# Expert weights in row chunks: up ahead of gate, accumulation over two chunks

## The reference, cut to what matters

```
def expert_block(args):
    ids, e = args
    xb = tokens_pad[ids]
    hgu = xb @ w_gu_l[e] + b_gu_l[e]
    gate = jnp.minimum(hgu[:, :D_EXPERT], SWIGLU_LIMIT)
    up = jnp.clip(hgu[:, D_EXPERT:], -SWIGLU_LIMIT, SWIGLU_LIMIT)
    act = gate * jax.nn.sigmoid(SWIGLU_ALPHA * gate) * (up + 1.0)
    return act @ w_dn_l[e] + b_dn_l[e]
```

## Time and profile before

| | us |
|---|---|
| median of 3 runs | 2111.39 (2110.61 to 2113.88) |
| the profiled execution | 2111.9 |
| its span | 2110.2 |
| first expert matmul | 780.1 |
| PE busy in the span | 1855.6 (88%) |
| DVE busy | 1531.5 (73%) |
| ACT busy | 1336.0 (63%) |

### The profile page before, as it was taken

How to read it: one execution, slowest core, us unless ns; L and a number is a source line. 1 busy time by engine, 2 the same in 40 slices (tenths; PEclk the granted TensorE clock), 3 DMA queues, 4 the chain that set the end, 5 groups by cost and what they waited for, 6 DMA issues and landing times.

```text
span 2110.2 us, 56858 instructions
## 1 busy us (share of the span) xinstructions
PE 1855.6 (88%) x23915; PEld 1646.0 (78%) x23915; DVE 1531.5 (73%) x1917; ACT 1336.0 (63%) x1751; POOL 309.8 (15%) x330
## 2 busy tenths in 40 slices
PE   5998898897779957899999999999999989899993
PEld 3585775575554547899999999999989989899893
DVE  5465566528862276788878887888888988989884
ACT  5354443227752244777777777778778787787883
POOL 2000000000000047311222122222221011111110
PEclk9999999999999959999999999999999999999996
DMA  6104111062124167899999999999999999999975
GB/s 187 39 25 128 31 31 35 26 174 67 61 99 163 60 251 276 272 305 327 316 337 328 336 315 336 343 340 350 349 344 349 365 363 358 367 354 366 362 236 180
DMA packets 246163, 503.91 MB, mean 239 GB/s; under 512 B 12967, under 2 KB 27603, under 8 KB 246017
## 3 DMA queue, kind: packets, MB, share of 16 engines
q1 hardware_dynamic: 228736, 459.91, 61.7%
q0 software_dynamic: 16192, 38.64, 7.5%
q10 hardware_dynamic: 1152, 4.19, 0.5%
HBM read 467.62 MB, written 37.38 MB: 239 GB/s over the span
## 4 chain that ended last, share of the span: by engine, by line
PE 61%; DVE 16%; issue 10%; ACT 8%; POOL 2%; DMA 2%; DVEq 0%; ACTq 0%; POOLq 0%; SPq 0%
PE PS L1577 34%; PE PS L1363 8%; PE PS L1369 6%; DVE RP L1192 5%; PE PS L1509 4%; PE PS L1415 4%; ACT RP L773 4%; DVE RW L1260 2%; ACT RT L809 2%; POOL table L555 2%; DVE RT L1274 1%; DVE RX L1070 1%; DVE RX L1105 1%; PE PS L1641 1%; DVE RW L1264 1%
## 5 line engine op out<-in xcount | busy, mean ns | idle before, releaser
L1577 PE MATMUL PS<-RT,RP 128*128 128x128 f16 (+3 forms) x18432 | 1130.2, 224 | 78.4 <-DVE RT L1274 59.3
L1577 PEld LDWEIGHTS PS<-RT,RP 128*128 128x128 f16 x18432 | 1120.5, 98 | 88.0 <-issue 67.0
L1192 DVE SCALAR_TENSOR_TENSOR RP<-RP 128x2048 f16<-128x2048 f32 x256 | 582.7, 2288 | 163.5 <-ACT RP L773 156.8
L773 ACT ACTIVATE RP<-RP 128x2048 f16<-128x2048 f32 x256 | 486.2, 1911 | 19.7 <-PE PS L1577 16.0
L1192 DVE SCALAR_TENSOR_TENSOR RP<-RX,RP 128x2048 f16<-128x2048 f32 x128 | 292.3, 2283 | 0.0
L773 ACT ACTIVATE RP<-RX 128x2048 f16<-128x2048 f32 x128 | 243.3, 1901 | 4.7 <-PE PS L1577 4.0
L1363 PE MATMUL PS<-RX,RW 128*128 128x512 f16 x768 | 172.7, 383 | 0.8 <-DVE RX L897 0.8
L663 ACT ACTIVATE RP<-PS 128x512 f32<-128x512 f32 (+1 forms) x56 | 33.3, 596 | 185.1 <-PE PS L1363 100.9
L1363 PEld LDWEIGHTS PS<-RX,RW 128*128 128x128 f16 x768 | 75.8, 99 | 87.3 <-issue 3.4
L804 ACT ACTIVATE RT<-RW 128x256 f16<-128x256 f32 (+3 forms) x128 | 55.3, 432 | 138.2 <-DVE RW L1268 134.1
L809 ACT ACTIVATE RT<-PS,bcur 128x128 f32<-128x128 f32 (+3 forms) x256 | 83.2, 384 | 84.5 <-PE PS L1577 83.5
(11 more groups left out here) (244 smaller groups left out, 1964.5 us busy)
## 6 DMA issues: line engine op xcount, KB each, us to landing
RP<-in_w_gate_up SPq DMA_DIRECT2D x128, 2048.0 KB
RX<-in_w_down SPq DMA_DIRECT2D x64, 2048.0 KB
RT<-in_w_in SPq DMA_DIRECT2D x28, 256.0 KB, 2.8
RQ<-in_w_in SPq DMA_DIRECT2D x28, 256.0 KB, 2.9
shifted_dram<-lrow_dram SPq DMA_DIRECT2D x8, 576.0 KB, 10.8
RP<-in_x SPq DMA_DIRECT2D x8, 512.0 KB, 5.3
RT<-RP SPq DMA_DIRECT2D x32, 128.0 KB, 2.3
RX<-shifted_dram SPq DMA_DIRECT2D x8, 512.0 KB, 3.6
```

What stands on the lines that cost most here:

```text
L773: act.activation(to[:, 0, 4 * h:4 * h + 4, :], src[:, 4 * h:4 * h + 4, :], ACT.Copy, scale=WS).then_inc(hi_done, 1)
L1192: dve.scalar_tensor_tensor(to[:, 1, 4 * h:4 * h + 4, :], src[:, 4 * h:4 * h + 4, :], WS, to[:, 0, 4 * h:4 * h + 4, :], ALU.mult, ALU.subtr ...
L1577: mm = pe.matmul(to, w[:, a, k, cols:cols + P], moving[:, b, k, :], start=(k == 0 and m == 0), stop=(k == KD - 1 and m == 2))
```

## The change

- The six chunks become 512 rows (four row blocks k) by 1024 columns: up (c = 0, 1), gate (2, 3), down (4, 5). A DRAM row of a chunk is then 4 KiB instead of 2 KiB long. `halve` works on the same number of elements, two row blocks by 1024 columns.
- PE takes the even chunk of a pair with k outside and the eight output tiles inside (`first_half`, counts `half_done`), then the odd chunk with the tile outside (`second_half`). So all eight tiles of up, of gate or of down accumulate over two chunks. They lie four to a bank for 128 tokens (two groups) and three to a bank for wide items (three groups of 3, 3 and 2 tiles: `groups`). `gu_done` and `dn_done` are counted once for each group.
- Up goes first. DVE clips the up tiles of a group (new lines 1267, 1272) while gate is being computed; then silu (811), product (1279), high part (818) and remainder (1285), each once for each group.
- Down starts on row block 0, which needs the first group of the activation alone, and needs the others later.
- `put_o` (823) copies out a whole group: four tiles, or three, three and two.
- ACT and DVE take their instructions in another order, below.

```diff
-            at = D * (c % 2) + 512 * (c // 2)
-            src = wg[:, :, at:at + 512] if c < 4 else wd[:, :, 512 * (c - 4):512 * (c - 3)]
+            k = 4 * (c % 2)
+            src = (wg[:, k:k + 4, D:2 * D], wg[:, k:k + 4, 0:D], wd[:, k:k + 4, :])[c // 2]
...
+        def groups(cap):
+            width = 4 if cap <= P else 3
+            return [range(f, min(f + width, KD)) for f in range(0, KD, width)]
...
+        def banks_of(cap):
+            return (0, 2, 4) if cap <= P else (0, 3, 0)
...
@@ ACT, halve @@
-                        if 3 <= c <= 6:
-                            act.wait_ge(gu_done, 8 * i + 2 * c - 4)
-                        if c == 7:
-                            act.wait_ge(dn_done, 4 * i + 2)
-                    act.activation(to[:, 0, 4 * h:4 * h + 4, :], src[:, 4 * h:4 * h + 4, :], ACT.Copy, scale=WS).then_inc(hi_done, 1)
+                        if c in (3, 5, 7):
+                            act.wait_ge(half_done, 3 * i + (c - 1) // 2)
+                        if c in (4, 6):
+                            act.wait_ge(gu_done, done_by(i, cap) + len(groups(cap)) * (c // 2 - 1))
+                    act.activation(to[:, 0, 2 * h:2 * h + 2, :], src[:, 2 * h:2 * h + 2, :], ACT.Copy, scale=WS).then_inc(hi_done, 1)
...
@@ ACT, the order in expert, behind halve(i, 2) @@
+                halve(i, 3)
+                halve(i, 4, cap=cap)
+                halve(i, 5, (0,))
                 act.wait_ge(bcur_ready, i + 1)
...
+                silu(0)
+                act_half(0)
+                silu(1)
+                act_half(1)
+                halve(i, 5, (1,))
+                for g in range(2, len(parts)):
+                    silu(g)
+                    act_half(g)
                 if more:
                     put_x(turned_by(i + 1, cap))
...
+                    halve(i, 6, cap=cap)
+                    halve(i, 7, (0,))
                 put_o(0)
                 if more:
...
                     halve(i, 7, (1,))
-                put_o(3)
+                for g in range(1, len(parts)):
+                    put_o(g)
...
@@ DVE, the order in expert @@
                 halve(i, 2)
                 halve(i, 3, (0,))
-                ups(0, 0)
+                ups(0)
                 halve(i, 3, (1,))
...
+                for g in range(1, len(parts)):
+                    ups(g)
+                halve(i, 4)
                 halve(i, 5, (0,))
...
+                for g in range(2):
+                    product(g)
+                    act_rest(g)
+                halve(i, 5, (1,))
+                for g in range(2, len(parts)):
+                    product(g)
+                    act_rest(g)
                 if more:
                     put_x(turned_by(i + 1, cap), cap)
...
@@ PE @@
+                first_half(0, up_at, x_now)
+                second_half(1, up_at, x_now, gu_done)
+                pe.wait_ge(o_rows, rows_by(i, cap) + 1)
+                first_half(2, gate_at, x_now)
+                second_half(3, gate_at, x_now, gu_done)
                 if more:
                     pe.wait_ge(xg_in, gathered_by(i + 2, cap))
...
+                first_half(4, down_at, act_now, [part[0] for part in parts])
+                pe.wait_ge(act_lo, groups_by(i + 1, cap))
+                second_half(5, down_at, act_now, dn_done)
```

More of the change, by code:

```diff
@@ L791, in expert @@
                 act.wait_ge(warmed, i + 1)
-                def silu(half, b):
-                    act.wait_ge(gu_done, 8 * i + 4 * half + b + 1)
-                    for f in range(2):
-                        k = 4 * half + 2 * b + f
-                        ins = act.activation(sig[b][:, f, 0:cap], PS[:, b, cap * f:cap * (f + 1)], ACT.Silu,
-                                             bias=bcur[:, k:k + 1], scale=ALPHA / WS)
-                    ins.then_inc(gate_free, 1)
-                def act_half(half, b):
-                    k = 4 * half + 2 * b
-                    act.wait_ge(act_f, 4 * i + 2 * half + b + 1)
-                    act.activation(actT[:, 0, k:k + 2, 0:cap], actf[b][:, :, 0:cap], ACT.Copy).then_inc(act_hi, 1)
@@ L806, in put_o, with silu @@
-                def put_o(q):
-                    act.wait_ge(dn_done, 4 * i + q + 1)
-                    for f in range(2):
-                        act.activation(oT[:, 2 * q + f, 0:cap], PS[:, 4 + q % 2, cap * f:cap * (f + 1)], ACT.Identity,
-                                       bias=bcur[:, 16 + 2 * q + f:17 + 2 * q + f], scale=1.0 / WS).then_inc(dn_free, 1)
+                _, gate_at, down_at = banks_of(cap)
+                parts = groups(cap)
+                def silu(g):
+                    act.wait_ge(gu_done, done_by(i, cap) + len(parts) + g + 1)
+                    for f in parts[g]:
+                        ins = act.activation(sig[:, f, 0:cap], expert_tile(gate_at, f, cap), ACT.Silu,
+                                             bias=bcur[:, f:f + 1], scale=ALPHA / WS)
+                    ins.then_inc(gate_free, 1)
@@ new lines, in act_half, with put_o @@
+                def act_half(g):
+                    f, end = parts[g][0], parts[g][-1] + 1
+                    act.wait_ge(act_f, groups_by(i, cap) + g + 1)
+                    act.activation(actT[:, 0, f:end, 0:cap], up[:, f:end, 0:cap], ACT.Copy).then_inc(act_hi, 1)
+                def put_o(g):
+                    act.wait_ge(dn_done, groups_by(i, cap) + g + 1)
+                    for f in parts[g]:
+                        act.activation(oT[:, f, 0:cap], expert_tile(down_at, f, cap), ACT.Identity,
+                                       bias=bcur[:, 16 + f:17 + f], scale=1.0 / WS).then_inc(dn_free, 1)
@@ L1571, in turn_x, with three @@
                     mm.then_inc(x_turned, 1)
-            def three(to, w, cols, moving, tiles=range(KD)):
-                for k in tiles:
-                    for m, (a, b) in enumerate(((0, 0), (0, 1), (1, 0))):
-                        mm = pe.matmul(to, w[:, a, k, cols:cols + P], moving[:, b, k, :],
-                                       start=(k == 0 and m == 0), stop=(k == KD - 1 and m == 2))
+            def three(to, w, f, k, moving, kk, first, final):
+                for m, (a, b) in enumerate(((0, 0), (0, 1), (1, 0))):
+                    mm = pe.matmul(to, w[:, a, k, P * f:P * (f + 1)], moving[:, b, kk, :],
+                                   start=(first and m == 0), stop=(final and m == 2))
                 return mm
@@ new lines, in expert, with weights_ready, first_half @@
+                parts = groups(cap)
+                def weights_ready(c, h):
+                    pe.wait_ge(hi_done, 12 * i + 2 * c + h + 1)
+                    pe.wait_ge(lo_done, 12 * i + 2 * c + h + 1)
+                def first_half(c, base, moving, act_groups=None):
+                    for k in range(4):
+                        if k % 2 == 0:
+                            weights_ready(c, k // 2)
+                        if act_groups is not None and k in act_groups:
+                            pe.wait_ge(act_lo, groups_by(i, cap) + act_groups.index(k) + 1)
+                        for f in range(KD):
+                            mm = three(expert_tile(base, f, cap), halved[c % 3], f, k, moving, k, k == 0 and f in [part[0] for part in parts], False)
+                    mm.then_inc(half_done, 1)
@@ new lines, in second_half @@
+                def second_half(c, base, moving, done):
+                    weights_ready(c, 1)
+                    for part in parts:
+                        for f in part:
+                            for k in range(4):
+                                mm = three(expert_tile(base, f, cap), halved[c % 3], f, k, moving, 4 + k, False, k == 3 and f == part[-1])
+                        mm.then_inc(done, 1)
+                pe.wait_ge(x_act, i + 1)
+                pe.wait_ge(x_dve, copied_by(i + 1, cap))
```

154 lines of the change are left out of this document (45 added, 109 removed).

## The result

The changed kernel takes 2168.02 us (median of four runs) against 2111.86 for the kernel before measured beside it: 1.0264 of it, 95% interval 1.0244 to 1.0284. That is 56 us slower, where 34 had been forecast (2145); the time lies in the stated range of 2109 to 2172. The profiled execution has a span of 2166.1 us against 2110.2. One of the four runs fell into the slow state, 2482.04 us at a mean granted clock of 0.741 where the other three have 0.95, and does not count in the ratio.

The account below looks back on a forecast made before the run. PE sets the pace, with DVE having only 4 to 9 us of slack an item; +6.4 (148 tokens), +21.6 (138), +7.8 and -2.7 (128) sum to +33.1, giving 2145 us, range 2109 to 2172.

Parts of the forecast that it names:

- what sets the end of an item: ACT and DVE chain delaying the output transposes: items of 38.2 against 37.53 us at 128 tokens, +2.5 us at 138.
- the steps on 512 elements: Product, high part and remainder on 512 elements: 0.69, 0.61, 0.69 us, between the present duration and twice it.
- the first and the last item of 128 lose their slow clock: With waits of 1.3 and 2.1 us the slow clock goes: -1.3 and -1.4 us.
- the clock: At 138 tokens, half clock behind a 2.8 us wait before the output transposes: +1.1 us in each of six items.
- behind 2.37 it stayed at 2.4 GHz, so 2.8 is on the costly side: PE waits: 2.37 us left the clock full, 2.73 and 3.05 halved it, so 2.8 at 138 tokens costs 1.6 us.
- rival D: Shorter waits behind down, or short runs of three matmuls, lower the clock in every other item: +42, 2187 us; chance 0.07.
- 148 tokens without the slow clock: Items of 148 tokens, end set by the chain of 19.7 us: 42.6 to 42.8 against 41.88 us, +6.4 over eight.
- Rival C: Loads were the hidden bound; longer rows save 2.5 us an item, 35 us over 14 items: 2076 us; chance 0.03.
- Rival B: ACT not late at item end, through 2 us sooner after the first high part: -21, 2090 us; chance 0.08.

Follow-up runs that it names:

- the fillers: Changed kernel with 16 to 40 matmuls that nobody reads put in front of PE's longest wait in each item: 2143.58 us, 1.0148 of before.
- one pair swapped on DVE: Changed kernel, items over 128 tokens only: third product and its remainder put ahead of DVE's last half of chunk 5: 2122.94 us, 1.0064 of before.
- the two orders together: Changed kernel with the instruction orders of ACT and DVE both changed, nothing else: 2055.70 us, 0.9728 of before.
- ACT's order alone: Changed kernel, ACT only: last half of chunk 5 behind first high part, next tokens before second, next chunk 0's first half before third: 2107.66 us.
- The last run: Kernel before with 34 matmuls that nobody reads between the two groups of output transposes at 128 tokens: 2133.88 us, 1.0099 of before.
- 2 KiB rows: Two DMAs per chunk, one for each half of its columns: changed kernel 2168.69 us; with ACT's and DVE's orders also changed, 2056.62 us.
- DVE's order alone: Changed kernel, DVE only: first product and remainder before chunk 5's first half, chunk 5's last half before second remainder: 2195.05 us, 1.0386 of before.
- with 20 and with 34 fillers: Kernel before with 20 or 34 unread matmuls between the two groups of output transposes at 128 tokens: 2116.59 and 2133.88 us.
- three groups at 128: Changed kernel with three tiles to a bank and three groups for items of 128 tokens too: 2215.06 us, 1.0493 of before.

## Why the prediction came out as it did

By its own parts (times of the profiled executions; the items run from the first expert matmul to the last transpose):

| | forecast | measured | given back by the fillers |
|---|---|---|---|
| 158, 4 items | 0 | +0.8 | 2.1 |
| 148, 8 items | +6.4 | +19.9 | 11.0 |
| 138, 6 items | +21.6 | +22.4 | 6.7 |
| 128, 14 items | +5.1 | +11.7 | 4.7 |
| start and tail | 0 | +1.1 | 1.0 |
| sum | +33.1 | +55.9 | 25.5 |

The 4.7 at 128 are 6.4 in the first 13 items, less 1.7 in the last.

**Right: what sets the end of an item.** The chain through ACT and DVE was read off the order and the durations. For 128 tokens it gave waits of 1.3, 0.3 and 1.9 us and an item of 38.2; the trace has 1.24, 0.37, 1.79 and 38.14. For 138 it gave the start of down at 24.5 us and of the output transposes at 39.7; they are at 24.3 and 39.8 (1488.65 and 1504.13 less 1464.35). One miss there is a wait of 1.05 in the middle of down, which was forecast as none; it costs nothing, since ACT, not PE, ends the item. Another is a slip in the sum: down from 24.5 on, at the 11.68 us of the earlier trace rows, ends at 36.2 and not at 36.9, so that the wait behind it would have been 3.5 us, not 2.8. It was 2.58, because down itself waited. The runs show the chain, not only fit it: one pair swapped on DVE gives 45 us, and the two orders together 112.

**Right: the steps on 512 elements.** Taken as 0.69, 0.61 and 0.69; measured 0.69, 0.63 and 0.69. Neither end of the range (0.42, 0.84) was near.

**Right: the first and the last item of 128 lose their slow clock**, and get shorter by 1.2 and 1.3 us (38.29 against 39.49; 37.04 against 38.38). For the last this was partly luck: with the same wait of 2.04 it did show the low clock in the fillers' run and with ACT's order alone (38.72 and 38.06 us).

**Wrong in size: the clock.** The step that failed is "behind 2.37 it stayed at 2.4 GHz, so 2.8 is on the costly side", which made a limit of length out of two lengths that the trace happened to show. It gave 6 x 1.1 us at 138 tokens, where 6.7 were measured; that agreement is luck, since the low clock came in four of the six and cost some 1.7 each time, with nothing hidden. And it gave nothing elsewhere. But behind waits of 2.20 at 148 it cost 11.0 us in eight items, and behind waits of 1.79 at 128 6.4 us in four. These 17.4 us of the 22.8 missed are part of what rival D priced at 42, with the clock in every other item too; it came in 14 of the other items, the first two among them, not in 26. The last run shows why two lengths of one trace were no basis: the wait of 2.38 costs nothing in twelve items of 37.53 us, and costs 1.6 us in six of twelve when the items are 38.4 us long. That 2168 still lies in the range is luck too: its upper end of 2172 was made for longer steps on 512 elements, which did not come, and the clock filled that room.

**Wrong by a little:** 148 tokens without the slow clock take 42.99, where 42.6 to 42.8 was worked out (2.5 us in eight items); 158 take 44.37, not 44.0.

**Rival C, the loads, is out**: 2 KiB rows change nothing, with items of 38 or of 36 us. The fear behind rival D, that short runs of three matmuls on one output tile lower the clock, is out too. The Trainium skill ("TensorE: Matmul & The Clock Gate", "A second HAM failure mode: psum-queue depth-cycling") warns of something near it, of cycling through PSUM banks in each iteration; here PE goes to another output tile every three matmuls and to another bank every nine or twelve in the first halves, and with both orders all items from the third to the thirty-first ran at 1.00. In the other kernels every lowering behind the second item followed a wait. **Rival B** (faster) had the right place, ACT after the first high part, and named the order against it; with the order mended the kernel is faster by 56 to 60 us, more than B's 21.

Not tried by themselves are up ahead of gate and the order with k outside in the first halves; that PE's own work took no longer with them is read from the trace alone (21.60 us for 384 matmuls, as before).

## What to carry to other kernels

Where two engines hand a tile back and forth, write down the order of both, and count for each handover what stands in front of it on the receiving side; a step moved on one engine alone may only move the wait, so try the pair. Work that is not yet due (here the chunk halves) belongs where its engine would otherwise stand, between giving something away and getting it back. And a change that looks lost can be an order that no longer fits it: here 1.026 of the time before became 0.972 without touching the new structure.

## What the runs showed of the hardware

- PE's clock falls to 1.2 GHz behind waits much shorter than the 2.73 us seen in the kernel before: in the changed kernel behind 2.20 with four transposes and 0.45 after it, in eight of eight items, behind 2.54 to 2.58, in four of six, and behind 1.79, in four of thirteen. Each time it cost 1.4 to 1.7 us.
- A length alone does not decide. Waits of 2.37 and 2.38 (one of them 2.43) were harmless in 12 of 12 items at 37.53 us an item, and costly in 6 of 12 at 38.4. The pair of 2.19 and 0.44 at 148 tokens, costly in 8 of 8 items of the changed kernel, was so in 4 of 8 with DVE's order alone. The longest, 3.05 and 3.06 in the last item, was costly in the kernel before and harmless with 20 and with 34 fillers. Only 2.72 to 2.74 (in three traces) and 2.97 (thirteen items, with three groups at 128) had the low clock behind them each time. That it is the moment at which a wait falls is what I take from this; the Trainium skill ("TensorE: Matmul & The Clock Gate", "What's actually happening") says that the chip's watch over TensorE runs freely and does not start anew with a kernel's work, and these runs agree. The fillers themselves are no explanation for all of it: the run with DVE's order has none, and in the changed kernel, which has none either, waits of 1.79 cost every third time; in the run with the third product earlier, whose items of 128 are the same and only begin at another time, five of the thirteen were long, not four. No run moved the start of a kernel's items and nothing else, so the moment as the cause is argued, not shown.
- Matmuls that nobody reads, put in a wait, keep the clock up: 24 us for 980 matmuls, in a kernel that is late for another reason. With the order mended there was nothing left for them to gain, since from the third item on none showed the low clock.
